# Conditioning by halves, the first expert pass's rows produced transposed, and idle products in TensorE's waits, in a hybrid diffusion step

## The reference

```python
sh1, sc1, g1, sh2, sc2, g2 = jnp.split(silu(cond) @ ada_w[layer] + ada_b[layer], 6, axis=-1)
h = rmsnorm(x, norm1_g) * (1 + sc1) + sh1
# layer 0: q, k, v, u = split(h @ na_w_in); neighbourhood/context attention on q, k, v; FFT mixing on u; @ na_w_out
# layer 1: gelu(h @ sg_w_in), spatial gating in chunks of 128, @ sg_w_out
x = x + g1 * mix
h = rmsnorm(x, norm2_g) * (1 + sc2) + sh2
x = x + g2 * moe(h)     # 16 experts of width 256, top 2 of one group of 4, router shared by the layers
```

## Time and profile before

| | us |
|---|---|
| three runs | 984.92, 987.49, 987.61 (median 987.49) |
| the profiled execution: its time | 983.97 |
| its span, first to last instruction | 982.2 |
| mean granted clock of TensorE over the span | 0.98 of full |

### The profile page before, as it was taken

The page is one execution under the profiler, slowest core; times in us unless marked ns, Lnnn a source line. Parts: engine busy times, 40 slices in busy tenths (PEclk is TensorE's granted clock), DMA queues, the critical chain, the costliest instruction groups (busy, mean ns, idle before and its releaser), DMA issues.

```text
span 982.2 us, 11471 instructions
## 1 busy us (share of the span) xinstructions
PE 919.2 (94%) x4284; PEld 436.1 (44%) x4284; DVE 493.3 (50%) x1034; ACT 181.8 (19%) x385; POOL 159.7 (16%) x162
## 2 busy tenths in 40 slices
PE   3799999988899989999997999999999989999997
PEld 1333345755545545443442443433645545434332
DVE  1643474157546767433335852872446767433336
ACT  5110100266411110111111611101211111111100
POOL 4011352048500001000004200010000001000013
PEclk9799999979999999999999899999999989999999
DMA  9967854572430167999988462644160167999967
GB/s 370 405 227 295 339 219 165 183 212 69 161 130 22 44 279 285 412 422 419 423 336 296 168 230 98 245 172 172 34 256 22 43 279 270 406 423 423 422 262 299
DMA packets 67981, 243.95 MB, mean 248 GB/s; under 512 B 7392, under 2 KB 22528, under 8 KB 49488
## 3 DMA queue, kind: packets, MB, share of 16 engines
q1 hardware_dynamic: 41616, 201.12, 51.9%
q0 software_dynamic: 8528, 27.99, 7.7%
q10 hardware_dynamic: 17776, 14.04, 4.7%
HBM read 215.01 MB, written 27.33 MB: 247 GB/s over the span
## 4 chain that ended last, share of the span: by engine, by line
PE 81%; DVE 7%; DMA 6%; issue 2%; ACT 1%; POOL 1%; SPq 0%; DVEq 0%; ACTq 0%; POOLq 0%
PE bank L2079 14%; PE bank L2067 14%; PE bank L2215 14%; PE bank L2048 8%; PE bank L2229 8%; PE bank L2019 4%; PE bank L2005 3%; DMA ring<-in_ada_w 3%; PE bank L2206 2%; PE bank L2118 2%; DMA ring<-in_moe_w_up 2%; DVE bz L1389 1%; DVE x_res L1389 1%; PE bank L2500 1%; PE bank L2565 1%
## 5 line engine op out<-in xcount | busy, mean ns | idle before, releaser
L2079 PE MATMUL bank<-ring,h_feat 128*128 128x512 f32 x320 | 145.3, 599 | 0.0
L2215 PE MATMUL bank<-ring,uv 128*32 128x512 f32 (+2 forms) x592 | 142.0, 594 | 3.4 <-ACT uv L1089 2.0
L2048 PE MATMUL bank<-ring,h_feat 128*128 128x512 f32 x176 | 82.3, 624 | 3.6 <-issue 1.8
L2079 PEld LDWEIGHTS bank<-ring,h_feat 128*128 128x128 f32 x320 | 58.0, 190 | 59.8 <-issue 59.7
L2215 PEld LDWEIGHTS bank<-ring,uv 128*32 128x32 f32 (+2 forms) x592 | 46.2, 128 | 69.8 <-issue 66.3
L1635 DVE TENSOR_TENSOR uv<-uv,bank 128x256 f32<-128x256 f32 x25 | 10.5, 421 | 128.4 <-ACT uv L1097 128.4
L2229 PE MATMUL bank<-ring,uv 128*32 128x512 f32 (+2 forms) x296 | 72.7, 596 | 1.2 <-issue 0.6
L2067 PE MATMUL bank<-ring,h_feat 128*128 128x512 f32 x144 | 63.9, 596 | 0.0
L2048 PEld LDWEIGHTS bank<-ring,h_feat 128*128 128x128 f32 x176 | 34.5, 200 | 48.8 <-issue 46.8
L954 POOL TENSOR_SCALAR h_tok<-h_tok 128x384 f32<-128x384 f32 (+1 forms) x40 | 44.2, 1118 | 62.6 <-DVE h_tok L1887 62.6
L978 POOL DMA_INDIRECT uv<-h_rows,small x23 | 21.8, 949 | 193.7 <-PE bank L2206 159.1
(11 more groups left out here) (310 smaller groups left out, 1348.3 us busy)
## 6 DMA issues: line engine op xcount, KB each, us to landing
bz<-in_ada_w SPq DMA_DIRECT2D x12, 2048.0 KB, 7.4
ring<-in_moe_w_gate SPq DMA_DIRECT2D x20, 1024.0 KB, 13.0
ring<-in_moe_w_up SPq DMA_DIRECT2D x20, 1024.0 KB, 15.3
ring<-in_moe_w_down SPq DMA_DIRECT2D x20, 1024.0 KB, 16.8
ring<-in_ada_w SPq DMA_DIRECT2D x8, 2048.0 KB, 15.1
h_tok<-in_moe_w_down SPq DMA_DIRECT2D x12, 1024.0 KB, 15.9
y_rows<-uv SPq DMA_DIRECT2D x23, 512.0 KB, 16.2
ring<-in_na_w_in SPq DMA_DIRECT2D x4, 2048.0 KB, 14.8
```

What stands on the lines that cost most here:

```text
L2048: last = mm(jbank(key)[:, :], HT[:, cc, P * t:P * (t + 1)], w[:, cc % 4, :], start=cc == 0, stop=cc == DC - 1)
L2079: last = mm(jbank(key)[:, :], HT[:, cc, P * t:P * (t + 1)], blk_ap(("out", layer, b))[:, cc, :], start=cc == 0, stop=cc == DC - 1)
L2215: last = mm(bank[2][32 * q:32 * (q + n), :], XT[:, b, cc, 32 * q:32 * (q + n)], w[:, :, cc, :], start=cc == 0, stop=cc == DC - 1)
```

## The change

Three parts.

1. **Conditioning split by output features (layer 0, group 0).** The first four blocks are now two halves of the output features, two blocks each (half the input features in each block). `first_ada_products(b)` multiplies one (16 matmul instructions with 256 columns each). After blocks 0 and 1 the shift and scale of features 0 to 511 are complete: `first_rows_half`, `mod_transposes(0, half)` and `set_first_half` finish one half, and chunks 0 to 3 of `HT` are modulated, then the same for chunks 4 to 7. `context_half(b, half)` is the context product over four chunks. The blocks are read in pieces of 2 KB in place of 8 KB, each with four DMAs; the two halves of the rows of `na_w_in`'s blocks 0 and 1 are loaded apart. ScalarE modulates two context chunks of each half, VectorE the other two (before: three and five of eight).
2. **First rows transposed.** `first_rows(t)` now has the rows of `H` stationary (every eighth feature) and the one-hot matrix moving: eight products of 128 columns in place of two of 512, which land in banks 0 and 1 in the layout of `XT`. `XG`'s copies and `xt_transposes(0)` are gone; two opening products of 512 columns of zeros clear the banks. `sum_groups(4)` moves ahead of `indices(3)`, and VectorE reads the first rows ahead of the indices.
3. **Idle products** (a result that nobody reads): one and two of 512 columns around the first half's transposes, one in each of the first two attention steps, three ahead of layer 1's `project(1, 2, 0)`.

```diff
-LOADS = [(("ada", 0, b), b) for b in range(4)]
+LOADS = [(("ada", 0, b), (2, 3, IN_BZ, SPLIT)[b]) for b in range(4)]
...
-BY_DVE = 5
+BY_DVE = 2
...
+        first_ada = ada_w[0].rearrange("(p b i) (g k h n) -> g h b p i k n", b=2, i=4, k=2, h=2, n=512)[0]
...
+            for b in range(2):
+                load_first_ada(b)
+            for b in range(2):
+                load_rows(b, 0)
+            load_first_ada(2)
+            sp.wait_ge(sumsq, TT)
+            load_first_ada(3)
+            for b in range(2):
+                load_rows(b, 1)
+            sp.wait_ge(ada_mm, 3)
             load_ada(0, 4)
-
-            sp.wait_ge(sumsq, TT)
+            sp.wait_ge(ada_mm, 4)
             load_ada(0, 5)
...
             read_transposes()
+            for h in range(2):
+                first_products("q", h)
             for n in range(2 * TT):
                 if n == 2:
-                    for h in range(2):
-                        first_products("q", h)
                     act.dma_start(mk.rearrange("p y k r -> p (y k r)"), mask).then_inc(act_in, 16)
...
-                dve.wait_ge(idx_mm, (TT + 2) * layer + TT)
-                nc.vector.tensor_copy(idx_sb, idx_all).then_inc(idx_ready, 1)
                 dve.wait_ge(xt_mm, NPASS * layer + 1)
                 nc.vector.tensor_copy(XT[:, 0, 4:8, :], bank[1][:, :].rearrange("p (c n) -> p c n", c=4))\
                     .then_inc(xt_dve, 1)
+                dve.wait_ge(idx_mm, (TT + 2) * layer + TT)
+                nc.vector.tensor_copy(idx_sb, idx_all).then_inc(idx_ready, 1)
...
+            def first_ada_products(b):
+
+                wait_block(pe, ("ada", 0, b))
+                s, half = place["ada", 0, b][0], b // 2
+                for i in range(4):
+                    pair = split_half(i // 2) if s == SPLIT else \
+                        block(s).rearrange("p c n -> p (c n)")[:, 2048 * (i // 2):2048 * (i // 2) + 2048]
+                    w = pair[:, 1024 * (i % 2):1024 * (i % 2) + 1024].rearrange("p (k j n) -> p j k n", k=2, j=4)
+                    cc = 4 * (b % 2) + i
+                    for j in range(4):
+                        out = ada_bank(0, 0)[32 * j:32 * j + 2, :].rearrange("p (u n) -> p u n", u=4)[:, half::2, :]
+                        last = mm(out, scond[:, :, cc], w[:, j], start=cc == 0, stop=cc == DC - 1)
+                last.then_inc(ada_mm, 1)
...
+            def idle_products(b, n):
+
+                for _ in range(n):
+                    mm(bank[b][:, :], ident, ident.unsqueeze(1).to_broadcast([P, 4, P]), start=True, stop=True)
...
-                    for half in range(2):
-                        last = mm(bank[half][:, :], first_oh[:, t, :], H[:, t, 512 * half:512 * half + 512],
-                                  start=t == 0, stop=t == TT - 1)
+                    for i in range(DC):
+                        last = mm(bank[i // 4][:, P * (i % 4):P * (i % 4) + P], H[:, t, i::DC], first_oh[:, t, :],
+                                  start=False, stop=t == TT - 1 and i % 4 == 3)
                     return last
...
-            ada(0, 0)
+            first_ada_products(0)
...
-            for cc in range(3):
+            for cc in range(DC):
                 latent_transposes(cc)
-            ada(0, 1)
-            for cc in range(3, DC):
-                latent_transposes(cc)
-            ada(0, 2)
-            ada(0, 3)
-            mod_transposes(0)
+            first_ada_products(1)
+            idle_products(6, 1)
+            mod_transposes(0, 0)
+            idle_products(6, 2)
...
+            context_half(0, 0)
+            first_ada_products(2)
+            context_half(1, 0)
+            first_ada_products(3)
+            pe.wait_ge(operands_set, H_LATENT[0])
+            product("q", 1, 0)
+            mod_transposes(0, 1)
+            product("q", 1, 1)
             for b in PAIR_BLOCKS["q"]:
-                wait_block(pe, ("in", 0, b))
-                project(0, b, 0)
+                context_half(b, 1)
                 ada_after(0, b, 0)
...
-            pe.wait_ge(mod1_set, 4)
+            pe.wait_ge(mod1_set, modulation_set(1))
             for v in range(PAIRS + PAIR_LAG + 1):
                 if v < PAIRS:
                     scores(v)
+                if v < PAIR_LAG:
+                    idle_products(7, 1)
...
+                    if t == 2:
+                        pe.wait_ge(x_out, 2)
+                        idle_products(7, 3)
                     wait_read(pe, ("tt", 0, 0))
```

More of the change, by code:

```diff
@@ L198, in plan_jobs @@
         add(("t", c), "act" if c % 2 else "dve")
+    for h in range(2):
+        add(("w", "q", 1, h), "act")
     for blk in PAIR_BLOCKS["q"]:
         add(("p", 0, blk, 0), "act")
-    for step in PRODUCTS:
+    for step in PRODUCTS[1:]:
         for h in range(2):
-            add(("w", "q", step, h), "act" if step == 1 else "dve")
+            add(("w", "q", step, h), "dve")
     for t in range(TT):
@@ L611, in build @@
             i = signal_of(s)
-            landed[i] += 2 if s == SPLIT or key in (("dft",), ("in", 1, 1)) else 1
+            landed[i] += 4 if key[:2] == ("ada", 0) and key[2] < 4 else 2 if s == SPLIT or key in (("dft",), ("in", 1, 1)) else 1
             place[key] = (s, landed[i])
@@ L1340, in finish_rows, with first_rows_half, set_first_half @@
                     nc.vector.scalar_tensor_tensor(scales, scales, 1.0, gains, ALU.add, ALU.mult).then_inc(fin_done, 1)
+            def first_rows_half(half):
+                rows, gains = side_rows(0, 0)
+                dve.wait_ge(side_in[0][0], 64)
+                dve.wait_ge(ada_mm, 2 * half + 2)
+                both = rows.rearrange("p (u n) -> p u n", u=4)[:, half::2, :]
+                link(nc.vector.tensor_tensor(both, ada_bank(0, 0)[:, :].rearrange("p (u n) -> p u n", u=4)[:, half::2, :],
+                                             both, ALU.add))
+                cols = slice(P * half, P * half + P)
+                scales = rows[:, 256:512][:, cols]
+                nc.vector.scalar_tensor_tensor(scales, scales, 1.0, gains[:, cols], ALU.add, ALU.mult).then_inc(fin_done, 1)
+            def set_first_half(half):
+                dve.wait_ge(modt_mm, half + 1)
+                for q in range(2):
+                    nc.vector.tensor_copy(mod1[:, 0, q, :, 4 * half:4 * half + 4],
+                                          bank[7][:, :].rearrange("p (u j r) -> p u j r", u=4, r=32)[:, half::2, :, q])\
+                        .then_inc(mod1_set, 1)
             def set_mod1(layer):
-                dve.wait_ge(modt_mm, 2 * layer + 1)
+                dve.wait_ge(modt_mm, 4)
                 for q in range(2):
@@ L2172, in out_projection @@
                 logits(TT - 1, 1)
-                indices(TT - 2)
-                sum_groups(TT - 1)
                 for h in range(2):
@@ L2177, in out_projection @@
                     wait_read(pe, ("r", layer, TT - 1, h))
+                sum_groups(TT - 1)
+                for half in range(2):
+                    open_first_rows(half)
+                indices(TT - 2)
                 for t in range(TT - 2):
@@ L2362, in ada_after, with context_half @@
                     ada(*ADA_AFTER[step])
-            pe.wait_ge(operands_set, H_CONTEXT)
-            pe.wait_ge(nonlinear_done, CONTEXT_SET)
+            def context_half(b, half):
+                key = ("p", 0, b, 0)
+                if half:
+                    wait_block(pe, ("in", 0, b))
+                else:
+                    job_free(pe, key)
+                    pe.wait_ge(block_in[b], 16)
+                pe.wait_ge(operands_set, H_CONTEXT[half])
+                pe.wait_ge(nonlinear_done, CONTEXT_SET[half])
+                for i in range(4):
+                    last = mm(jbank(key)[:, :], HT[:, 4 * half + i, 0:P], row_half(("in", 0, b), half)[:, i, :],
+                              start=half == 0 and i == 0, stop=half == 1 and i == 3)
+                if half:
+                    last.then_inc(job_done, 1)
+            context_half(0, 0)
[6 more added lines that the diff above has]
+            product("q", 1, 1)
             for b in PAIR_BLOCKS["q"]:
-                wait_block(pe, ("in", 0, b))
-                project(0, b, 0)
+                context_half(b, 1)
                 ada_after(0, b, 0)
-            pe.wait_ge(operands_set, H_LATENT)
-            for step in PRODUCTS:
+            ada_after(0, "q", 1)
+            pe.wait_ge(operands_set, H_LATENT[1])
+            for step in PRODUCTS[1:]:
                 for h in range(2):
```

118 lines of the change are left out of this document (63 added, 55 removed).

## The result

The changed kernel takes 998.96 us (median of 4 runs, 995.53 to 1002.1) against 987.24 for the kernel before on the same chip (984.92 to 987.61). The ratio is 1.0123, 95% interval 1.0086 to 1.016. I had forecast 976 and a range that ended at 983. The profiled execution took 999.19 us, its span is 997.4.

The account below looks back on a forecast made before the run. TensorE, busy 94% of the span, was taken as the bound. Gains 5.5 + 1.8 + 0.9 + 1.4 + 0.3 = 9.9 us gave 974.1 from the profiled time, 977.6 from the median; forecast 976, range 969.5 to 983.

Parts of the forecast that it names:

- eight are 1.83 per token tile ... So nothing: First expert pass: eight 128-column products per token tile take 1.83 us against 1.84 for two of 512, no added cost.
- read with a stride: First rows' products: 40 different weights per layer might not overlap, about 22 us more in all, 998 us; chance 0.03.
- Start, 5.5 us: Layer 0's conditioning start: 7.3 us lead, less 0.5 for late transfers and 1.3 for block 6; from 2 to 8.
- I take 1.3: Start, block 6 sharing DMA with the mask and bias table: TensorE's wait, between 0 and 2.5 us, charged at 1.3.
- The rule on transposes: Start: by the skill, 40 transposes together would leave the clock low; by the profile row they do not.
- Pairs, 1.8: Attention pairs' start: idle products keep TensorE's clock full, gaining 1.8 us, from -0.5 to 3.
- Experts, 0.9 and 1.4: First expert passes: gain of 0.9 us in layer 0 (-0.4 to 1.3) and 1.4 in layer 1 (0.9 to 1.8).
- The mechanism that I named: First expert pass: `indices(4)` covers ScalarE's copy, so `gate_up` follows 1.2 us behind the end of `first_rows(4)`.
- Layer 1's start, 0.3: Layer 1's start: idle products bring the clock back sooner but delay the product; gain 0.3 us, from -1.5 to 1.6.
- The sum: Whole kernel: gains of 5.5, 1.8, 0.9, 1.4 and 0.3 make 9.9 us; forecast placed at 976 us.

## Why the prediction was wrong

The step that failed is in part 2: "eight are 1.83 per token tile ... So nothing". I priced a product of 128 columns by the earlier trace rows, four products whose weights lie side by side in SBUF, and the diff says `H[:, t, i::DC]`, every eighth float. The term was 0.115 us for each of 80 records, and 0.241 was measured: 10.1 us more per layer, 20 in all, which turns a gain into the 12 us of loss. I did name the step as a rival ("read with a stride", 998 us) and gave it 0.03, because the spacing of 0.11 in the earlier trace rows "speaks against it"; it speaks only of consecutive floats. The rival's time was right by luck, and its mechanism was not: the records do overlap, a load of 335 ns every 241. A row that could have made me ask was in the trace of before, though not among those I showed: the transposes of L2206, which read every eighth float, load their weights in 194 ns, those of L2005 with consecutive floats in 141:

```profile
L2206 PEld LDWEIGHTS bank<-small,uv 128*128 128x128 f32 x200 | 25.0, 194 | 11.6 <-issue 11.6
...
L2005 PEld LDWEIGHTS bank<-small,uv 128*128 128x128 f32 x40 | 4.6, 141 | 0.7 <-DVE uv L1986 0.3
```

I took transposes for a kind of their own and did not ask why. The row would not have given the size: those transposes stand 0.12 us apart all the same. The Trainium skill's rule on lines of 16 bytes, cited above, speaks against this change too, and I had not looked for it.

The other steps, in their order:

- **Start, 5.5 us.** The lead ahead of block 6 was forecast at 7.3 and measured at 8.2 (first context half at 29.35, forecast 30.4; block 2 awaited for 0.42, forecast 0.5). Of the difference 0.8 is block 0: I had it land at 16.5, later than before, for its small pieces, and it was used at 15.66. The term "I take 1.3" for block 6 was mis-sized: it landed 11.8 after its issue, worse than its upper bound of 11.0, the wait was 3.08, and the clock fell behind it for another 1.7, which I had not counted at all. Instead of 5.5, 3.3 were left; with the table later, 8.2.
- **The rule on transposes.** The 40 transposes run from 19.18 to 24.56, and the clock comes up at 20.86, in the midst of them, and stays full to 68.65. Two stretches of that time (length, busy time by engine, granted clock, DMA share, GB/s):

```profile
20.90:29.00 8.10, 8.10 (x74) 5.32 (x72) 6.39 (x12) 4.87 (x7) 0.00 (x0) 1.00 1.06 367
38.00:58.00 20.00, 20.00 (x101) 7.74 (x99) 13.88 (x19) 4.13 (x8) 0.33 (x1) 1.00 0.89 328
```

  As forecast by the row, transposes don't keep the clock low; that goes against the rule of the Trainium skill (TensorE: Matmul & The Clock Gate, Part 4: PE-mode transpose) that the prediction names. Whether they raise it this doesn't show: a product at half clock (15.66 to 19.18) ran just ahead of them.
- **Pairs, 1.8.** Right in place and size at first: full clock from 199 on, and the lead grows from 3.3 to 5.2 at 245.70. Then a half-clock stretch from 246.14 to 249.56 took 1.6 back, with TensorE busy all through it. Six of the other ten kernels have it at that place, within 5 us, the one without idle products among them; the version with the second part undone has none. What brings it stays open.
- **Experts, 0.9 and 1.4.** Apart from the step, no gain is to be seen. From the folding of tile 3 to `gate_up` it was 26.04 us before, with 3.4 of half clock in it, so 24.3 without; it is 24.70 at full clock with every second float, and 28.50 with 10.2 of half clock, so 23.4 without, with consecutive ones. That leaves anything from 0.4 lost to 0.9 won. The mechanism that I named holds (`gate_up` stands right behind the late indices, forecast 1.2 after the end of L2182, measured 1.0), but the opening products, 1.97 us, stand in the path, where I had put them into a wait of VectorE's.
- **Layer 1's start, 0.3.** In the changed kernel -5.8 before it and -5.6 behind it, as forecast. Without the second part the same idle products kept the clock full and were worth 2.0.
- **The sum** of the forecast, 976, is that of the parts that worked: 977.02 with the second part undone and the table moved. That is two errors of mine taken out, not a forecast that held.

## What to carry to other kernels

Price an operand by its step in bytes, not by its shape alone: here floats 16 bytes apart as weights, and 32 bytes apart as weights or as moving operand, cost TensorE's float32 products twice the time of neighbours, and a transpose with the same step next to nothing, so that a layout which saves a transpose can cost more than it. Moving the step to another engine only moves the price, so ask where that engine stands in the path. When a start is drawn together, list each transfer that is issued relative to it: the bias table, harmless before, cost more than half of the lead.

## What the runs showed of the hardware

- TensorE, float32, products of 128x128 by 128: loads take 192, 196, 330 and 335 ns at steps of 4, 8, 16 and 32 bytes; the records stand 0.114, 0.120, 0.236 and 0.241 us apart. With the moving operand at a step of 32 bytes: loads of 208 ns, 0.234 us apart.
- VectorE, float32, 128x1024, two operands: 1.28 and 1.23 us with neighbours, 2.08 us where both operands are read with a step of 32 bytes, 2.02 where one is.
- The transposes ahead of the later passes load in 194 ns with a step of 32 bytes, and in 143 once the features are permuted; between 388 and 437 us eight of them take 1.05 to 1.16 us with the step and 1.04 to 1.09 without it.
- Two transfers of 2 MB issued 1.5 us apart from two queues: the one issued second (block 6) landed after 11.8 us in place of 7.3, the first after 18.1.
